# Moving the second bf16 remainders of h1 behind the norm, in 256-column pieces on GpSimd

## The reference, cut to what matters

```
a  = token_mix(h)                         # retention and convolution branches
h1 = layer_norm(ALPHA * h + a, ln1)       # [320, 1024], float32
g  = softmax(h1 @ w_rg + b_rg);  e = h1 @ w_re + b_re      # 4 groups, 8 experts in each
top-1 group, top-2 experts in it, combine weights
m  = sum over the chosen experts: (silu(h1 @ w_eg) * (h1 @ w_eu)) @ w_ed
pe = (p @ w_proj) * sigmoid(h1 @ w_gate)
y  = layer_norm(ALPHA * h1 + m + pe, ln2)
```

## Time and profile before

| | us |
|---|---|
| median of 3 runs | 921.92 |
| lowest and highest | 920.5, 921.98 |
| profiled execution | 920.81 |
| its span | 918.3 |
| PE busy in the span | 859.0 (94%) |
| DVE busy | 383.2 (42%) |
| ACT busy | 294.6 (32%) |
| POOL busy | 76.1 (8%) |

### The profile page before, as it was taken

One profiled execution on the slowest core, in us unless ns is written; L12 is line 12 of the kernel. 1 busy time (PEld: TensorE's weight loads), 2 busy tenths in 40 slices (PEclk: granted clock), 3 DMA queues, 4 the chain that ended last, 5 costly groups with the idle time before them and its releaser, 6 DMA issues.

```text
span 918.3 us, 15455 instructions
## 1 busy us (share of the span) xinstructions
PE 859.0 (94%) x6336; PEld 536.0 (58%) x6336; DVE 383.2 (42%) x720; ACT 294.6 (32%) x333; POOL 76.1 (8%) x82
## 2 busy tenths in 40 slices
PE   7999998999999899899999999998999899989875
PEld 5998777789998797654444434443444353434321
DVE  7599998897675265761111110101010131010127
ACT  3332234666547833243132222212222222111110
POOL 1100000011110000323010000000000000000000
PEclk9999998999999999889999999999999999999997
DMA  9744437659997747818999999999999999999971
GB/s 344 263 156 132 166 117 214 176 155 254 216 269 228 183 182 321 367 46 293 420 418 420 421 421 421 420 420 423 422 419 422 423 421 420 421 420 421 421 273 57
DMA packets 42786, 284.87 MB, mean 310 GB/s; under 512 B 6602, under 2 KB 6858, under 8 KB 9456
## 3 DMA queue, kind: packets, MB, share of 16 engines
q1 hardware_dynamic: 35888, 254.25, 69.4%
q0 software_dynamic: 6560, 27.82, 12.7%
q10 hardware_dynamic: 288, 2.10, 0.5%
HBM read 258.51 MB, written 13.13 MB: 296 GB/s over the span
## 4 chain that ended last, share of the span: by engine, by line
PE 51%; DMA 28%; DVE 4%; ACT 2%; issue 2%; SPq 1%; ACTq 0%; POOLq 0%; DVEq 0%
DMA raw_x<-wstream 25%; PE ps L1560 13%; PE ps L1289 5%; PE ps L1291 5%; PE ps L1290 5%; PE ps L1580 4%; PE ps L1507 4%; PE ps L1537 3%; PE ps L1321 2%; DMA y_tok<-y_sb,dest 1%; DMA y_second<-y_tok 1%; PE ps L1322 1%; PE ps L1323 1%; PE ps L1316 1%; PE ps L1331 1%
## 5 line engine op out<-in xcount | busy, mean ns | idle before, releaser
L1560 PE MATMUL ps<-raw_x,xs 128*64 128x512 f32 x1024 | 233.8, 598 | 24.1 <-DMA raw_x<-wstream 24.1
L1560 PEld LDWEIGHTS ps<-raw_x,xs 128*64 128x64 f32 x1024 | 71.0, 136 | 140.1 <-issue 137.7
L909 DVE SCALAR_TENSOR_TENSOR cT_sb<-uT_sb,conv_par,cT_sb 128x350 f32<-128x350 f32 x240 | 120.7, 578 | 0.7
L1580 PE MATMUL ps<-raw_x,actT 128*64 128x512 f32 x512 | 115.4, 592 | 0.0
L558 ACT ACTIVATE w_hi<-raw_dense 128x2048 fp32r<-128x2048 f32 x41 | 78.3, 1911 | 75.0 <-PE ps L1316 41.1
L1289 PE MATMUL ps<-hT_hi,w_hi 128*128 128x320 f32 x304 | 96.7, 318 | 0.9 <-issue 0.9
L1290 PE MATMUL ps<-hT_lo,w_hi 128*128 128x320 f32 x304 | 94.7, 312 | 0.0
L1072 DVE TENSOR_TENSOR onehot<-iota_r,rankm 128x192 bf16<-128x192 f32 x33 | 11.8, 357 | 179.2 <-PE ps L1537 179.2
L1537 PEld LDWEIGHTS ps<-onehot,h1b 128*128 128x128 bf16 x2304 | 69.1, 98 | 25.7 <-issue 25.7
L1291 PE MATMUL ps<-hT_hi,w_lo 128*128 128x320 f32 x256 | 79.9, 312 | 0.0
L1580 PEld LDWEIGHTS ps<-raw_x,actT 128*64 128x64 f32 x512 | 36.8, 137 | 72.7 <-issue 71.1
(11 more groups left out here) (274 smaller groups left out, 1082.1 us busy)
## 6 DMA issues: line engine op xcount, KB each, us to landing
raw_x<-wstream SPq DMA_DIRECT2D x192, 1024.0 KB, 23.4
raw_dense<-wstream SPq DMA_DIRECT2D x43, 1024.0 KB, 5.8
w_lo<-raw_dense POOLq DMA_DIRECT2D x11, 1024.0 KB, 8.6
w_lo_third<-raw_dense POOLq DMA_DIRECT2D x6, 1024.0 KB, 9.6
y_tok<-nothing POOLq DMA_DIRECT2D x2, 1280.0 KB, 7.7
ln_gb<-ln POOLq DMA_DIRECT2D x2, 1024.0 KB, 8.1
raw_dense<-wstream ACTq DMA_DIRECT2D x2, 1024.0 KB, 12.7
const<-consts SPq DMA_DIRECT2D x1, 1297.5 KB, 15.1
```

The source lines that it names most:

```text
L909: i = stt(out=cT[:, j, :], in0=src, scalar=w, in1=cT[:, j, :], op0=ALU.mult, op1=ALU.add)
L1560: i = mm(ps[64 * h:64 * h + 64, 1 + odd, :], x, w[h][:, k, :], start=half == 0 and k == 0, stop=half == 1 and k == 3)
L1580: i = mm(ps[64 * h:64 * h + 64, 4 + par, :], a, w[:, f, h, :], start=j == 0 and f == 0, stop=j == 1 and f == 1)
```

## The change

The first remainders of all three tiles are now made on VectorE, after the norm of the last tile. The second remainders stay on GpSimd, but all of them come after the last `h1_rows` and the DMA to `ln_gb`, and each is four instructions of 256 columns. ScalarE makes all second parts, and then all third parts, after the last `h1T_copy`. The arithmetic is the same.

```diff
 # GpSimd
-        def rest(t):
-            pool.wait_ge(ss("part_hi"), t + 1)
-            sub(part_tmp[t][:], rows[:, t, :], h1b[:, 0, t], ALU.subtract).then_inc(ss("rest_pool"), 1)
         def rest_2(t):
             pool.wait_ge(ss("part_mid"), t + 1)
             src = part_tmp[t] if t < 2 else wide
-            sub(src[:], src[:], h1b[:, 1, t], ALU.subtract).then_inc(ss("rest_pool"), 1)
-        pool.wait_ge(ss("pe_done"), SPLIT)
-        rest(0)
-        rest_2(0)
-        rest(1)
+            for c in range(4):
+                c = slice(256 * c, 256 * c + 256)
+                m = sub(src[:, c], src[:, c], h1b[:, 1, t, c], ALU.subtract)
+            m.then_inc(ss("rest_pool"), 1)
         pool.wait_ge(ss("h1_rows"), TILES)
         pool.dma_start(ln_gb[:], ...)
-        rest_2(1)
-        rest_2(2)
+        for t in range(TILES):
+            rest_2(t)
 # ScalarE
         def mid_part(t):
-            if t < 2:
-                act.wait_ge(ss("rest_pool"), 2 * t + 1)
-            else:
-                act.wait_ge(ss("rest_dve"), 1)
+            act.wait_ge(ss("rest_dve"), t + 1)
         def last_part(t):
-            act.wait_ge(ss("rest_pool"), 2 * t + 2 if t < 2 else 5)
+            act.wait_ge(ss("rest_pool"), t + 1)
         root(2)
-        mid_part(0)
         hi_part(1)
         h1T_copy(1)
         hi_part(2)
         h1T_copy(2)
-        last_part(0)
-        mid_part(1)
-        mid_part(2)
-        last_part(1)
-        last_part(2)
+        for t in range(TILES):
+            mid_part(t)
+        for t in range(TILES):
+            last_part(t)
 # VectorE
         layer_norm(ln_gb, "ln1_in", "h1_rows", wide, merge_begin)
-        dve.wait_ge(ss("part_hi"), TILES)
         dve.wait_ge(ss("h1_rows"), TILES)
-        tt(wide[:], rows[:, 2, :], h1b[:, 0, 2], ALU.subtract).then_inc(ss("rest_dve"), 1)
+        for t in range(TILES):
+            dve.wait_ge(ss("part_hi"), t + 1)
+            tt((part_tmp[t] if t < 2 else wide)[:], rows[:, t, :], h1b[:, 0, t], ALU.subtract).then_inc(ss("rest_dve"), 1)
         route()
```

## The result

The changed kernel took 914.97 us in the median of 8 runs (911.53 to 917.87), the kernel before 920.22 in the same comparison (8 runs); the ratio is 0.9937, 95% interval 0.9919 to 0.9955, so 4.1 to 7.5 us faster. The profiled execution took 916.86 us, span 914.8, against 920.81 and 918.3.

What follows compares the result with a forecast made beforehand. The prediction took the expert stream's speed and restart as the bound, TensorE and the norm deciding the restart. Profiled 920.81 less 1.83 gave 918.98, or 920.1 us on the median's footing; range 918.0 to 922.3.

Steps and rivals of the forecast that it cites:

- The way to the end: Expert weight stream: restarting it earlier by x brings the end forward by x, if it then never stops.
- Part 1: Norm of tiles 1 and 2: without GpSimd work beside it, VectorE's passes lose 4.60 us; TensorE gains 1.83 us.
- Gain for TensorE: TensorE's waits before the transposes of tiles 1 and 2 go: 0.99 + 0.84 = 1.83 us.
- the other 2.8 us of the norm's 4.6: Norm time saved beyond TensorE's 1.83 us of waits; claimed to buy nothing directly.
- The rival of the early clock: TensorE's clock rises during the first gate records; gain 3.4 us, to 918.5 us; chance 0.20.
- Part 2: Three first remainders on VectorE after the norm: 3.7 us, done at 390.2 before the logits; cost nothing.
- Part 3: ScalarE's second parts after tile 2's transposed copy: 1.06 us at most; GpSimd may start near 391.95.
- Part 4: GpSimd's twelve pieces beside VectorE's routing: 0.60 us each, alternating, holding routing 2.4 us; price 0.
- Just hidden: Routing done at 403.2 us, TensorE ready for the rank matmuls at 403.45; 0.25 us of cover left.
- The slower rival: Fixed cost per GpSimd instruction, 0.95 us a piece: routing late, about 3.2 or 1.7 us slower; chance 0.08.

Runs made afterwards that it cites:

- fillers: The kernel before with extra matmuls on constants in TensorE's gaps: five of them 920.08 us, eleven of them 919.16 us.
- warm_gaps: The kernel before with five extra 256-column matmuls on constants in TensorE's gaps; 920.08 us, ratio 0.9995.
- hot_before: The kernel before with eleven extra 256-column matmuls on constants, leaving TensorE no gap over 0.42 us; 919.16 us, ratio 0.9986.
- again: The changed kernel run again with no edit; 915.47 us, ratio to the kernel before 0.9948.
- whole: The changed kernel with whole 1024-column second remainders on GpSimd in place of the four pieces; 917.17 us, ratio to the kernel before 0.9967.
- split: The changed kernel with tile 0's second part earlier on ScalarE and its second remainder on VectorE while that waits for logits; 915.49 us, ratio to before 0.9961.
- best: Not defined by name in the text; apparently the repeat of split_warm beside the change: 915.65 us, ratio to the kernel before 0.9952.
- split_warm: The changed kernel with split's edit plus two extra matmuls on constants after tile 0's transposes; 913.59 us, ratio to the kernel before 0.9935.

## Why the prediction was wrong, step by step

- **The way to the end**: right. Stretch and median moved together: means of the traces 26.79 - 22.28 = 4.51 us; the ratios of the change's three comparisons say 4.8 to 5.8, their intervals 2.9 to 7.5, and the bare medians differ by 3.7 to 5.3. Whether anything beyond the stretch adds to the gain stays open.
- **Part 1, the norm**: right to 0.01 us (4.59 for 4.60).
- **Part 1, "Gain for TensorE: 0.99 + 0.84 = 1.83 us at the clock of before"**: this step failed. The gaps were read as if TensorE's own time beside them were fixed. It was not: at half clock TensorE came late to the norm's edge, and the gap was short. Before, T0 to T2 is 11.89 us whatever the clock, as the fillers show (the wait grew to 2.89 us in warm_gaps). With the norm out of the way T0 to T2 is TensorE's own, 9.27 us in the mean and 7.36 with the clock up all along (0.15 us of it a wait for tile 1's norm). That is 2.62 us in the mean for the 1.83, and 3.23 (11.90 less 8.67) in the first traces of the two kernels. So the sentence that the other 2.8 us of the norm's 4.6 buy nothing failed with it.
- **The logits**: not in the sum at all. I took from T2 to the sixteen gate records to be what it was. It fell from 6.19 to 4.09 us in the mean, 2.10 more: wholly at the low clock the logits' sixteen records take 3.61 us on a tile of 128 rows and 1.90 on tile 2, at the high one 1.95 and 1.10. After the change the logits of tiles 1 and 2 mostly meet the high one: in four of six traces the clock didn't fall in them at all, in all four of before it did. That this comes of the gate's records running without a gap before them is likely but not shown; in hot_before the clock fell in the last logits without such a gap.
- **The rival of the early clock** had the right mechanism at a chance of 0.20 and a gain of 3.4 us. In four of six traces of the change the sixteen gate records ran wholly at full clock, with stretches 4.2 to 4.6 us under the first trace of before. Its 3.4 us still lacked the logits. The same goes for the range: its lower end was this rival, less 0.5. The profiled execution of before was moreover among its shorter stretches (26.01, mean 26.79), which the forecast couldn't see from one trace but should have allowed for.
- **Part 2**: right. VectorE was done with the remainders at 390.40, 2.0 us before the logits.
- **Part 3**: right. ScalarE's second parts didn't hold GpSimd up beyond what was foreseen: it started 2.4 us after tile 2's transposes (390.66 less 388.28), against 2.65 foreseen.
- **Part 4**: the piece cost 0.63 us (0.60 taken), the engines alternate, the lock took 2.5 us (2.4 taken). "Just hidden" was true only at the low clock: in again TensorE is last, in four traces it waits 1.67 or 1.68 us for routing. As the rule of the Trainium skill (GPSIMD Engine Reference, 2.1 "Instruction dispatch") was applied, the lock would have been held across pieces; the run with whole ones shows that it is let go at the seam, so the measurement decides against that use of it.
- **The slower rival** fell with the 0.63 us (its 3.2 us were 408.4 less 405.28, so 3.1); the strided L464 was no guide to a contiguous piece.

## What to carry to other kernels
A gap of an engine isn't what the wait costs when that engine's own clock moves in the stretch: ask when the released producer comes, and lay the consumer's work out again at both levels of the clock. Here work on GpSimd beside two-input VectorE operations was paid for by VectorE, so put it where VectorE waits, or cut it so that each turn is short. And where the clock moves within the stretch, one trace is a sample: take the term's spread from several before narrowing a range.

## What the hardware showed beyond that
- GpSimd's float32 subtraction of 256 columns takes 0.63 us in a row of such, 1024 columns 2.11: (4 x 0.63 - 2.11) / 3, about 0.14 us for each further instruction. A waiting two-input operation of VectorE runs at the seam between two of them: at 394.47 in whole, and at every piece in the change.
- In the dense part, far from the change, the clock fell in some executions and not in others with the same instructions. Windows of TensorE, the change's first trace and then split:
```profile
140.00:160.00 20.00, 17.42 (x90) 0.83 0.83 209
```
```profile
140.00:160.00 20.00, 17.42 (x102) 1.00 0.87 215
```
Across this stretch the weight copies of split (w_hi<-raw_dense on ScalarE) went from 0.5 to 3.5 us ahead of those of the change's first trace, and what follows went with them: tile 0's transposes start at 375.61 and 379.61 us. Over all traces that start lies between 375.43 and 381.54 us, and the three shortest profiled executions (split, best and split_warm, 910.11 to 911.64 us) are the three where it lies below 377. So a part of the scatter of the times comes from ahead of the stretch, and spans such as split's 908.1 say nothing about its edit.
